# A hybrid decoder block on one Trainium2 core: the order of scores, weighted sums and the spreading in the attention loop

## The reference, cut to what matters

```
s = einsum('bqhd,bkhd->bhqk', q[:, q0:kend], k[:, :kend]) * scale
s = s + c[:, :, q0:kend, None] - c[:, :, None, :kend]
mask = (kpos[None, :kend] <= qpos[:, None]) & (kpos[None, :kend] >= PAD)
p = softmax(where(mask, s, NEG_INF), axis=-1)
out = einsum('bhqk,bkhd->bqhd', p, v[:, :kend])
```

## Time and profile before

| | us |
|---|---|
| median of 3 runs | 2862.14 (2860.37 to 2864.8) |
| the profiled execution: time | 2878.77 |
| its span, first to last instruction | 2876.9 |
| the attention loop in it | about 842 to 1304 |

### The profile page before, as it was taken

The page is one execution under the profiler, slowest core; times in us unless marked ns, Lnnn a source line. Parts: engine busy times, 40 slices in busy tenths (PEclk is TensorE's granted clock), DMA queues, the critical chain, the costliest instruction groups (busy, mean ns, idle before and its releaser), DMA issues.

```text
span 2876.9 us, 40988 instructions
## 1 busy us (share of the span) xinstructions
PE 2799.6 (97%) x14586; PEld 2066.1 (72%) x14586; DVE 1707.1 (59%) x4617; ACT 621.4 (22%) x1276; POOL 1347.0 (47%) x1140
## 2 busy tenths in 40 slices
PE   8999999999999999998999989999999999999997
PEld 4488888888876666664555767878878777787765
DVE  6655656657347777773777445677677772323226
ACT  2222222210025555551101101011111111111115
POOL 3533434547731111111455245677667665565535
PEclk9999999999999999999999999999999999999999
DMA  6500010111121113006444357899899989999986
GB/s 223 188 6 17 15 46 1 30 30 30 44 64 38 62 40 134 25 29 241 151 144 154 125 223 227 257 290 278 270 281 286 283 278 296 307 301 311 316 248 253
DMA packets 192573, 470.52 MB, mean 164 GB/s; under 512 B 27384, under 2 KB 108104, under 8 KB 166632
## 3 DMA queue, kind: packets, MB, share of 16 engines
q1 hardware_dynamic: 145424, 347.63, 33.8%
q0 software_dynamic: 44640, 111.84, 16.7%
q10 hardware_dynamic: 2304, 8.39, 0.7%
HBM read 349.64 MB, written 118.11 MB: 163 GB/s over the span
## 4 chain that ended last, share of the span: by engine, by line
PE 39%; DMA 7%; POOL 3%; DVE 3%; issue 2%; SPq 1%; ACT 0%; POOLq 0%; DVEq 0%; ACTq 0%
PE ps L3067 18%; PE ps L2842 7%; PE ps L3015 4%; DMA moe_xg<-t_rows,index 4%; PE ps L2986 3%; PE ps L2898 3%; DMA base_rows<-moe_yo,index 3%; PE ps L2983 2%; DVE moe_xT L2143 1%; POOL moe_xg L2569 1%; PE ps L2908 1%; POOL base_rows L2590 1%; PE ps L2861 1%; POOL moe_fin L2651 1%; PE ps L2852 0%
## 5 line engine op out<-in xcount | busy, mean ns | idle before, releaser
L2569 POOL DMA_INDIRECT moe_xg<-t_rows,index x433 | 426.7, 985 | 173.9 <-issue 133.8
L3067 PEld LDWEIGHTS ps<-moe_xT,moe_wg 128*128 128x128 f32 x2048 | 352.4, 196 | 56.6 <-issue 36.8
L3067 PE MATMUL ps<-moe_xT,moe_wg 128*128 128x192 f32 (+22 forms) x2048 | 379.6, 338 | 11.3 <-DVE moe_hh L2043 8.3
L3067 PE MATMUL ps<-moe_xT,moe_wu 128*128 128x192 f32 (+22 forms) x2048 | 376.7, 337 | 0.0
L2590 POOL DMA_INDIRECT base_rows<-moe_yo,index x100 | 229.2, 2292 | 278.3 <-DVE moe_yo L2157 99.0
L2143 DVE STREAM_TRANSPOSE moe_xT<-moe_xg 128x256 f32<-128x256 f32 x433 | 235.2, 609 | 207.6 <-DMA moe_xg<-t_rows,index 190.8
L3067 PEld LDWEIGHTS ps<-moe_xT,moe_wu 128*128 128x128 f32 x2048 | 354.4, 197 | 4.9
L2706 ACT ACTIVATE moe_sl<-ps 128x256 f32<-128x256 f32 (+19 forms) x144 | 49.6, 345 | 946.6 <-PE ps L3067 763.9
L1342 POOL TENSOR_TENSOR fox_diag<-fox_c,fox_causal 128x128 f32<-128x128 f32 x128 | 55.7, 456 | 417.1 <-DVE fox_mx L1371 412.3
L1365 DVE CUSTOM_DVE_ANT_0 hT<-ps,fox_c 128x512 f32<-128x512 f32 (+7 forms) x320 | 166.5, 560 | 77.4 <-PE ps L1634 77.2
L2198 DVE SCALAR_TENSOR_TENSOR moe_yo<-ps,weight,moe_yo 128x512 f32<-128x512 f32 (+14 forms) x280 | 187.4, 740 | 26.9 <-ACT moe_yo L2729 20.9
(11 more groups left out here) (376 smaller groups left out, 5013.2 us busy)
## 6 DMA issues: line engine op xcount, KB each, us to landing
moe_wg<-in_we_gate SPq DMA_DIRECT2D x64, 1024.0 KB
moe_wu<-in_we_up SPq DMA_DIRECT2D x64, 1024.0 KB
moe_wd<-in_we_down SPq DMA_DIRECT2D x64, 1024.0 KB
fox_c<-ck SPq DMA_DIRECT2D x8, 1032.0 KB, 8.8
emb_xin<-in_x SPq DMA_DIRECT2D x16, 512.0 KB, 3.9
h_rows<-emb_hr SPq DMA_DIRECT2D x16, 512.0 KB, 2.8
ret_w<-in_w_in SPq DMA_DIRECT2D x16, 512.0 KB, 6.6
moe_yt<-h_rows SPq DMA_DIRECT2D x16, 512.0 KB
```

What stands on the lines that cost most here:

```text
L2569: pool.indirect_dma_start(out=xg[g % NXG][:, :], out_offset=None, in_=quarters, in_offset=bass.IndirectOffsetOnAxis(ap=route.index4[:, AT4 ...
L3067: ins = pe.matmul(out, w[:, c, f:FF:FC], xT[u][:, c, 0:n], start=(c == 0), stop=(c == DC - 1))
```

## The change

In each round of the attention loop the scores move in front of the weighted sums on TensorE. The spreading moves from behind the group's last weighted sum to behind its first. On ScalarE `keep` moves in front of the round's `exps_last`. On VectorE `finish` moves behind the round's `bias`. No instruction is added or removed, and no DMA; their order on three engines changes.

```
@@ vector
                     if i == (2 if HALF[n] else 0) and len(groups[n]) > 1:
                         inverse(n)
-                    if i == len(groups[n]) - 1 and i >= 1:
-                        finish(n)
                     for m, u in (scores_in[n, i] if ROUNDS[n] > 1 else []):
                         bias(m, u)
-                    if len(groups[n]) == 1 and i == 0:
+                    if i == len(groups[n]) - 1:
                         finish(n)
@@ scalar
                     if i == ROUNDS[n] - 1 and n + 1 < NT:
                         for s in groups[n + 1][0]:
                             back(n + 1, s)
+                    if len(groups[n]) > 1 and i == spread_at[n]:
+                        keep(n)
                     for m, q, a in exps_last.get((n, i), ()):
                         exps(m, q, a)
-                    if len(groups[n]) > 1 and i == spread_at[n]:
-                        keep(n)
@@ tensor
+                    for m, u in scores_in[n, i]:
+                        scores(m, u)
                     for s in (groups[n][i] if i < len(groups[n]) else []):
                         weigh(n, s)
-                    if i == spread_at[n]:
-                        scatter(n)
-                    for m, u in scores_in[n, i]:
-                        scores(m, u)
+                        if i == spread_at[n] and s == groups[n][i][0]:
+                            scatter(n)
```

## The result

The changed kernel takes 2919.5 us (median of 4 runs, 2919.27 to 2921.2) against 2861.3 us (2859.77 to 2864.8): a ratio of 1.0191, interval 1.0179 to 1.0204. It is slower by 58 us. The forecast was 2908, in a range of 2882 to 2924; the rival in which the granted clock falls as well was put at 2921, and that is the one that came. The ratios in this document are the record's own estimate over its runs; they differ from the quotient of the two medians (here 1.0204) by up to 0.15%. One execution of all that were timed, of 6553 us in e3_keep_alone, is left out as disturbed.

A forecast was written before the change was run, and what follows sets the result against it. TensorE was taken to bound the attention loop. Waits for copy and exponentials 35.8, VectorE's biases 8.6, 3-step tiles 1.5 and the end -0.4 sum to 45.5 us; on 2862.1 that gives 2908 us, range 2882 to 2924.

The forecast's parts named there:

- the rival in which the granted clock falls as well: Idle TensorE at four 17-step tile ends drops its clock, costing 13 us more: 2921 us, chance 0.2.
- the end: At the very end of the loop `keep` no longer stands behind the last sum: -0.4 us.
- The bound: TensorE sets the end of the attention loop, with 11.2 of 438 us idle; each new wait is paid in full.
- all else runs back to back: Apart from first transposes (4.8 us) and spreading (1.6 us), TensorE was said to wait for nothing in the loop.
- The copy in front of the spreading: In 15-, 13-, 11- and 9-step tiles the spreading waits for ScalarE's last-step copy: 0.73 us in 16 tiles, 11.7 us.
- `keep` in front of the exponentials: The next tile's exponentials wait for `keep`, its first transposes for them; with the copy's wait, 35.8 us over four pairs.
- The exponential's length plus 0.34: Delay of the next tile behind 15-, 11- and 9-step tiles: 1.93, 1.51 and 1.28 us, the copy's 0.73 included.
- VectorE's late third copy: VectorE's copy waits for the first sum behind the scores, delaying biases and TensorE's next scores: 8.6 us over four pairs.
- `finish` at nothing: `finish` behind the biases on VectorE costs nothing, its result being due only after a block of transposes (1.5 us).
- the sign by which the prediction itself said that it would be wrong: A granted clock below 1.00 in the attention loop would show the forecast wrong.
- The waits cover each other: The exponentials' share vanishes; only the copy and the biases are paid, 20.3 us: 2882 us, chance 0.12.
- faster: Scores in front end all of TensorE's waits in the loop, 11.2 us: 2851 us, chance 0.04.

The follow-up runs named there:

- e3_keep_alone: The kernel before, with `keep` in front of the exponentials on ScalarE as the only change: +13.7 us, ratio 1.0052.
- e11_six_keep_behind_all: The changed kernel with six buffers `pT` instead of five and `keep` behind the exponentials in every tile, the 3-step one included: -6.1 us, ratio 0.9984.
- e6_scores_finish: The kernel before, with only the scores in front of the weighted sums and `finish` behind the biases: +24.1 us, ratio 1.0090.
- e12_finish_alone: The kernel before, with `finish` behind the biases on VectorE as the only change: +19.1 us, ratio 1.0066.
- e2_spread_behind_last: The changed kernel, with the spreading again behind the group's last sum: +77.9 us against the kernel before, ratio 1.0262.
- e1_keep_behind: The changed kernel, with `keep` back behind the round's exponentials on ScalarE: +21.6 us against the kernel before, ratio 1.0078.
- e5_fill_matmul: The changed kernel, with three extra float32 matmuls in front of the wait behind each 17-step tile: +46.8 us against the kernel before, ratio 1.0173.
- e9_fill_transpose: The changed kernel, with 24 extra float32 transposes in front of the wait behind each 17-step tile: +47.6 us against the kernel before, ratio 1.0165.

## Why the prediction was right, point by point

Per tile, the growth from one tile's first transposes to the next one's, in the change with the wait filled (so without falls), summed over the four pairs, beside the prediction's terms:

| behind the | forecast | measured (with the falls) |
|---|---|---|
| 17-step tiles | 8.0 + VectorE 5.3 | 10.9 (10.9) |
| 15-step tiles | 7.7 + VectorE 3.3 | 11.4 (19.6) |
| 13-step | 2.9 | 3.3 (3.4) |
| 11-step | 6.0 | 7.0 (6.7) |
| 9-step | 5.1 | 5.6 (5.3) |
| 7-step | 3.2 | 3.7 (3.3) |
| 5-step | 2.9 | 3.0 (2.7) |
| 3-step | 1.5 | 3.6 (3.3) |
| the end | -0.4 | -0.4 (-0.4) |
| sum | 45.5 | 48.1 (54.8) |

*The bound.* That each new wait of TensorE in the loop is paid in full held: its idle time rose from 13.8 to 56.0 us over the loop and its busy time from 459.6 to 472.2, which makes the whole 54.8. Of the 12.6 more that it was busy, 9.1 are gone in the run filled with matmuls (474.5, of which 11.4 are the filling); the other 3.5 were not followed up. The sentence "all else runs back to back" was wrong, though: in the same 438 us the second halves of three 17-step tiles waited as well (TensorE's groups over 866 to 1304 us):

```profile
L1660 PE MATMUL ps<-ident,hT 128*16 128x128 f32 x12 | 3.0, 275 | 1.5 <-ACT hT L1528 1.5
```

*The copy in front of the spreading.* 0.73 in 16 tiles was forecast. It is 0.84, the handover from ScalarE's copy to TensorE being 0.14 and not 0.05 (1026.26 to 1026.40). No row gave the 0.05; the rows had 0.15 from ScalarE's exponential to TensorE (983.70 + 1.80 to 985.65), which the same sum uses further on. The run with the spreading alone shows the mechanism by itself, the one with six buffers shows that the buffer count makes it.

*`keep` in front of the exponentials.* "The exponential's length plus 0.34" held in the change within 0.16 us for each tile: 2.08 behind the 15-step tiles (1023.40 to 1029.10 is 5.70, against 3.62), 1.67 behind the 11- and 1.33 behind the 9-step ones, against 1.93, 1.51 and 1.28. With the wait filled the last two are 1.75 and 1.41. The wait behind the 17-step tiles was forecast at 2.14 more, with VectorE 3.5 for a whole tile, and the whole tile came out at 2.81. The wait itself grew by 2.11, from 1.07 to 3.18. What was missed are the waits of L1660 shown above, 0.51 us each: the delay behind the 3-step tile in front of them now covers them. On the other side the 3-step tile costs 1.1 and not 0.5, more than the 0.9 that was its upper end. Its `keep` stood in front of the exponential already before, and with it behind the tile takes 0.66 less than before (e11_six_keep_behind_all). The two errors, about 0.6 each, cancel, which is luck.

*VectorE's late third copy.* In round 0 of a 15-step tile, where 0.8 was forecast, the timeline of the change reads:

```profile
1013.66 1.66 PE L1678 MATMUL ps<-fox_pT,fox_v 16*64 16x256 f32 x12
...
1014.42 0.69 DVE L1395 COPY fox_pT<-ps 128x512 f32<-128x512 f32 x1 [1.92 <-PE ps L1678]
...
1015.23 0.88 DVE L1406 TENSOR_SCALAR fox_rd<-ident,fox_rinv 128x128 f32<-128x128 f32 x4
...
1015.25 1.53 PE L1653 MATMUL ps<-ident,hT 128*128 128x128 f32 x12
...
1017.38 0.48 PE L1632 MATMUL ps<-fox_qk 64*128 64x128 f32 x3 [0.60 <-DVE fox_mx L1365]
```

The copy starts 0.76 behind the first sum, reciprocal and products follow, and the scores wait for L1365 until 1017.38, 0.60 us of it idle. In the whole loop there are 11 such waits in the tiles, 2.4 us in the 15-step and 3.9 us in the 17-step ones, 6.3 us where 8.6 was forecast; with six buffers there is none. (The prediction's 2898 to 2918, "nothing, or twice as large", is 2899 to 2916 by its own 8.6.)

*`finish` at nothing.* Right in the change, and for the reason given: 0.6 us before and after. But it is free only with the scores in front. Alone it is 21 us. The prediction named two covers: the tile's last sum comes behind the scores, and a block of transposes lies in front of the next tile's first sum. This run takes away the first alone, and the 18.9 us of waits show that the block of transposes doesn't suffice.

*The clock.* This is the step that failed. The likeliest case was put at 2908 without falls, and 0.2 was given to the one with them, at 2921. The argument against was that 1.6 us of idle time behind the first tile had left the clock at 1.00. A wait of 3.18 us didn't leave it there: the clock fell at all four places, and the loop's mean of 0.98 is the sign by which the prediction itself said that it would be wrong. That took 8.2 us, not 13: two of the four falls lasted 3.4 us, and part of the time at half clock TensorE was waiting anyway. The range held because the rival was in it. That the rival's 2921 lies so near to 2919.5 is in part luck: by its terms the loop would be 45.5 + 13 = 58.5 us longer. It was 54.8, made of 48.1 without falls (2.6 more than the sum) and 6.7 for them, and 3.5 us that are not in the loop came on top.

*The other rivals.* "The waits cover each other" (2882) and "faster" (2851) didn't come. Idle time of ScalarE in the loop rose and helped nobody, as the chain starts in its own round.

## What to carry to other kernels

The same swap on one engine cost 12 us of loop or 34, and a part that was free in the change cost 21 by itself: what an in-order engine may wait for depends on what the engine that waits for it has between. So a change of order is priced as a chain, from the event that releases the first waiter to the one that is needed last, and against the work that still lies beside it, and not part by part. A wait on an output queued in front of work for the next stage is the dangerous pattern. And where the sum leaves TensorE idle for longer at one place than anything in the trace of before, that its clock held there says nothing of the new wait: the fall belongs in the forecast itself.

## What the runs showed of the hardware that was not expected

- The granted clock fell from 2.4 to 1.2 GHz, for 3.4 or 6.8 us, at idle stretches of TensorE inside a busy loop, but the same wait didn't always bring a fall. Three of the four falls in the change began while TensorE still stood idle (at 872.05 in the wait from 870.02 to 873.20, for one); others began up to 1.3 us behind the wait. At the 3.18 us waits it fell at four places of four in the change and at three of four with six buffers; at waits of 2.3 us once in four (e3_keep_alone) and six times in seven (e6_scores_finish); at 2.50 us once in three (e12_finish_alone); and in e2_spread_behind_last at all eleven of 4.05, 2.35 and 2.05 us. Shorter waits brought a fall twice: one of 1.21 us near the start of the loop with six buffers (the fall at 844.05), and one of 1.38 us near the end of e2_spread_behind_last (1372.67 to 1374.05, the fall at 1374.28), where three waits of the same length brought none. Waits of 1.40, 1.64, 1.69 and 1.78 us (e1_keep_behind, the kernel before, e5_fill_matmul) brought none either. What decides between like waits stays open.
- Float32 transposes hold the clock as matmuls do (e9_fill_transpose against e5_fill_matmul, both without a fall).
- From the end of ScalarE's copy to TensorE's next matmul it takes 0.14 us (1026.26 to 1026.40), while VectorE begins 0.03 us behind ScalarE's copy (1303.37 to 1303.40, the last tile before).
